# First softmax attention of a two-block transformer kernel: TensorE's order of work, item by item against two items at a time

## The reference, cut to what matters

```python
def sliding_window_attention(q, k, v, sinks):
    # 8 heads of 64 in q, 2 in k and v; blocks of 128 queries; block n sees key blocks n-1 and n
    scores = jnp.einsum('bnqhgd,bnkhd->bnhgqk', qb, kb).astype(jnp.float32) * (Dh ** -0.5)
    scores = jnp.where(valid[None, :, None, None], scores, -jnp.inf)
    m = jnp.maximum(jnp.max(scores, axis=-1, keepdims=True), sink)
    e = jnp.exp(scores - m)
    denom = jnp.sum(e, axis=-1, keepdims=True) + jnp.exp(sink - m)
    probs = (e / denom).astype(v.dtype)
    out = jnp.einsum('bnhgqk,bnkhd->bnqhgd', probs, vb)
```

## Time and profile before

| | us |
|---|---|
| three runs | 2562.1, 2562.7, 2562.7 (median 2562.7) |
| span of the profiled execution, first to last instruction | 2561.3 |
| what lies around the span (median less span) | 1.4 |
| PE busy in the span | 2541.6 |
| DVE busy in the span | 1596.4 |
| ACT busy in the span | 912.6 |
| the stage changed: first scores to last value products | 434.78 to 494.93 |
| mean granted TensorE clock | 1.000 |

### The profile page before, as it was taken

The page is one execution under the profiler, slowest core; times in us unless marked ns, Lnnn a source line. Parts: engine busy times, 40 slices in busy tenths (PEclk is TensorE's granted clock), DMA queues, the critical chain, the costliest instruction groups (busy, mean ns, idle before and its releaser), DMA issues.

```text
span 2561.3 us, 31974 instructions
## 1 busy us (share of the span) xinstructions
PE 2541.6 (99%) x12548; PEld 2107.0 (82%) x12548; DVE 1596.4 (62%) x1976; ACT 912.6 (36%) x1184; POOL 10.2 (0%) x24
## 2 busy tenths in 40 slices
PE   8999999999999999999999999999999999999999
PEld 7888888778888888877898888888886888888887
DVE  6444468866444468677765747476357665775755
ACT  5222234543222245344443423233146343432322
POOL 0000001000000000000000000000000000000000
PEclk9999999999999999999999999999999999999999
DMA  5222233112222232212321232323210232232222
GB/s 182 102 83 99 96 110 120 67 50 96 103 89 98 99 115 101 99 50 99 132 94 63 104 103 82 115 83 123 94 66 13 87 116 83 84 115 83 101 96 82
DMA packets 37410, 241.91 MB, mean 94 GB/s; under 512 B 4416, under 2 KB 7280, under 8 KB 9136
## 3 DMA queue, kind: packets, MB, share of 16 engines
q1 hardware_dynamic: 34736, 233.78, 26.3%
q10 hardware_dynamic: 1920, 5.22, 0.6%
q0 software_dynamic: 640, 1.31, 0.2%
HBM read 236.89 MB, written 2.10 MB: 93 GB/s over the span
## 4 chain that ended last, share of the span: by engine, by line
PE 93%; DVE 5%; ACT 1%; issue 1%; DMA 0%; POOL 0%; DVEq 0%; ACTq 0%
PE ps L605 24%; PE ps L607 24%; PE ps L606 24%; PE ps L1234 1%; PE ps L623 1%; PE ps L625 1%; PE ps L624 1%; PE ps L766 1%; PE ps L1267 1%; PE ps L1291 1%; PE ps L1282 1%; DVE w_lo L2048 1%; PE ps L768 1%; PE ps L767 1%; PE ps L1303 1%
## 5 line engine op out<-in xcount | busy, mean ns | idle before, releaser
L605 PE MATMUL ps<-op_hi,w_hi 128*128 128x512 f32 x2056 | 800.9, 390 | 0.2 <-DVE op_lo L1929 0.2
L606 PE MATMUL ps<-op_lo,w_hi 128*128 128x512 f32 x2056 | 800.5, 389 | 0.0
L607 PE MATMUL ps<-op_hi,w_lo 128*128 128x512 f32 x2056 | 800.4, 389 | 0.0
L1350 ACT ACTIVATE w_hi<-w_raw 128x2048 fp32r<-128x2048 f32 x217 | 414.4, 1911 | 485.2 <-PE ps L607 315.3
L2048 DVE TENSOR_TENSOR w_lo<-w_raw,w_hi 128x2048 fp32r<-128x2048 f32 x217 | 497.0, 2292 | 38.7 <-ACT w_hi L1350 22.3
L605 PEld LDWEIGHTS ps<-op_hi,w_hi 128*128 128x128 f32 x2056 | 386.3, 188 | 81.4 <-issue 1.4
L607 PEld LDWEIGHTS ps<-op_hi,w_lo 128*128 128x128 f32 x2056 | 386.2, 188 | 80.6
L606 PEld LDWEIGHTS ps<-op_lo,w_hi 128*128 128x128 f32 x2056 | 386.3, 188 | 80.3
L2013 DVE SCALAR_TENSOR_TENSOR x<-ps,x 128x512 f32<-128x512 f32 x134 | 92.7, 691 | 310.8 <-PE ps L607 293.0
L605 PE MATMUL ps<-h_hi,w_hi 128*128 128x512 f32 x692 | 269.5, 389 | 0.0
L606 PE MATMUL ps<-h_lo,w_hi 128*128 128x512 f32 x692 | 269.2, 389 | 0.0
(11 more groups left out here) (373 smaller groups left out, 3085.7 us busy)
## 6 DMA issues: line engine op xcount, KB each, us to landing
w_raw<-in_wstream_dram SPq DMA_DIRECT2D x217, 1024.0 KB, 4.8
cr_m<-in_mem_dram ACTq DMA_DIRECT2D x2, 1024.0 KB, 4.9
w_raw<-in_wstream_dram SPq DMA_DIRECT2D x7, 256.0 KB, 8.0
x<-in_x_dram SPq DMA_DIRECT2D x3, 512.0 KB, 7.3
out_dram<-x SPq DMA_DIRECT2D x3, 512.0 KB, 2.6
m_s<-m_q POOLq DMA_DIRECT2D x16, 64.0 KB, 2.5
ev_s<-in_alibi_dram ACTq DMA_DIRECT2D x1, 1024.0 KB, 4.9
m_c<-in_rope_dram ACTq DMA_DIRECT2D x1, 640.0 KB, 3.9
```

The lines of the kernel that those rows point to most:

```text
L605: mm_(o, w_hi[:, c % 4, w], hi[:, k, 0:cols], start=(k == 0), stop=False)
L606: mm_(o, w_hi[:, c % 4, w], lo[:, k, 0:cols], start=False, stop=False)
L607: mm = mm_(o, w_lo[:, c % 4, w], hi[:, k, 0:cols], start=False, stop=(k == kt - 1))
L1350: f_(w_hi[:, c % 4, :], w_raw[:, c % 2, :], ACT.Copy).then_inc(w_hi_ready, 1)
```

## The change

PE's order in this attention alone is replaced. It takes the items in pairs: the score products of items i and i+1 in one run, then the masks of both, then the turns of item i-2, an eighth of a slab, the turns of item i-1, the next eighth, and last the value products of items i-2 and i-1 in one run. The scores of a pair wait until the exponentials of both items before are done. The eighth of step 18 follows at the end. The program of DVE, ACT, POOL and SP is unchanged, and so is the number of instructions of each kind on PE. The other user of `attention` (the differential attention) keeps its order.

```diff
-                    if i not in late:
-                        between(i)
+                    between(i)
...
-                    if i in late:
-                        between(i)
+                n["it"] += N
+
+            def attention_by_pairs(slabs, items, score_parts, p_blocks, outputs, turn_bank, between):
+
+
+                i0, N = n["it"], len(items)
+                pe.wait_ge(rs_used, n["job"])
+
+                def turn(i):
+                    pe.wait_ge(p_ready, i0 + i + 1)
+                    if i == 0:
+                        pe.wait_ge(acc_free, slabs + 2)
+                    else:
+                        pe.wait_ge(pt_copied, i0 + i)
+                    for b, src in enumerate(p_blocks(i0 + i, *items[i])):
+                        mm = nc.tensor.transpose(ps[:, turn_bank, b * P:(b + 1) * P], src, ident)
+                    mm.then_inc(pt_ready, 1)
+
+                for i in range(0, N + 2, 2):
+                    if i < N:
+                        if i:
+                            pe.wait_ge(e_ready, i0 + i)
+                        pair = [score_parts(i + a, *items[i + a]) for a in range(2)]
+                        for parts in pair:
+                            for o, l, r, _ in parts:
+                                mm_(o, l, r, start=True, stop=False, skip_group_check=True)
+                        for parts in pair:
+                            for o, _, _, bias in parts:
+                                mm = mm_(o, ident_r[:], bias, start=False, stop=True, skip_group_check=True)
+                            mm.then_inc(s_ready, 1)
+                    if i:
+                        turn(i - 2)
+                    between(i)
+                    if i:
+                        turn(i - 1)
+                    between(i + 1)
+                    if i:
+                        for a in range(i - 2, i):
+                            pe.wait_ge(pt_copied, i0 + a + 1)
+                            outputs(i0 + a, *items[a])
                 n["it"] += N
...
-            attention(AT_MIX1 + MIX1_FIRST, SLIDE_ITEMS, slide_scores, slide_blocks, slide_out, [2],
-                      slide_between, late=(8, 16))
+            attention_by_pairs(AT_MIX1 + MIX1_FIRST, SLIDE_ITEMS, slide_scores, slide_blocks, slide_out, 2,
+                               slide_between)
+            slide_between(len(SLIDE_ITEMS) + 2)
```

More of the change, by code:

```diff
@@ L801, in eighth_positions, with attention @@
                     mm.then_inc(slab_done, 1)
-            def attention(slabs, items, score_parts, p_blocks, outputs, turn_banks, between, scored=None, late=()):
+            def attention(slabs, items, score_parts, p_blocks, outputs, turn_banks, between, scored=None):
                 i0, N, T = n["it"], len(items), len(turn_banks)
```

## The result

The changed kernel takes 2572.2 us (median of 5 runs, 2571.7 to 2573.1), the kernel before 2562.7 (2561.6 to 2562.9): ratio 1.0039, 95% interval 1.0027 to 1.0051. It is 9.5 us slower, 10.4 were forecast.

What follows compares the result with a forecast made beforehand. PE is nearly full, with DVE working off a backlog; pairing makes each pair one trip through PE, DVE and ACT. The stage ends 10.4 us later: 2561.3 + 10.4 = 2571.7 span, plus 1.4 gives 2573.1 us, range 2567 to 2577.

Steps and rivals of the forecast that it cites:

- What bounds the stage: In the changed stage, PE runs ahead and DVE follows with a backlog, waiting for scores only 4.4 us in all.
- 5.0 us of changes of shape: On PE alone in the stage, shape changes fall from 9.6 to 4.6 us, a gain if PE's order set the pace.
- rival A: Faster: PE sets the pace in the stage and DVE loses at most its 4.4 us of waits; 2558.3 us, chance 0.05.
- The new dependency: PE scores a pair only after the products of i-1, needing ACT's copy after the exponentials of i+1; DVE's backlog goes.
- The loop's terms: One pair's trip through PE, DVE and ACT: 7.19 us for four-block pairs, 6.65 with a one-block item first.
- plain pair: A four-block pair without other work in its loop: one trip through three engines, 7.19 us.
- other work inside the loop: DVE's work at even steps and ACT's `high` lengthen their pairs, by 0.72 to 2.25 us a piece.
- The loop's start: First pair starts at 434.78, second at 441.20 after item 1's exponentials; PE waits 2.3 us there.
- Nothing later has a known slack: Behind the stage nothing absorbs the delay, so the levels and all after run some 10 us later.
- rival C: Slower still: PE, idle more, is granted 1.2 GHz through the stage; 2609 us, chance 0.03.
- second loop of nearly the same length: The turn of i-1, waiting for the copy of i-2, closes another loop, within 0.2 us; up to 1.4 more in total.
- Rival B: No difference that can be told: DVE's idle 7.1 us behind the stage takes up lateness; 2566.0 us, chance 0.06.

Runs made afterwards that it cites:

- products_by_two: The kernel before, item order kept, with only the value products taken two items in a row at every second step: 2561.3 us, ratio 0.9998.
- wait_only: The kernel before, item order kept, with scores of an even item waiting for the exponentials of the item just before: 2568.2 us, ratio 1.0022.
- products_later: The changed kernel with a pair's value products moved behind the next pair's scores: 2566.6 us, ratio 1.0017.
- change_filled: The changed kernel with 34 unread matmuls of 512 columns added in PE's waits: 2572.4 us, ratio 1.0039.
- besides_odd: The changed kernel with three pieces of DVE's other work moved one step later, out of the loop: 2569.6 us, ratio 1.0030.
- dve_by_pairs: The changed kernel with DVE by pairs too, probabilities of i-1 first, then the maxima of i and i+1: 2568.7 us, ratio 1.0025.
- all_by_pairs: The changed kernel with DVE ordered by pairs, ACT's other work moved, and value products behind the next pair's scores: 2563.5 us, ratio 1.0004.
- masks_apart: The changed kernel with each item's masks right behind its own scores, sixteen more changes of shape: 2572.5 us, ratio 1.0038.

## Why the prediction was right, point by point

- **What bounds the stage.** Right. The 5.0 us of changes of shape were PE's to win and DVE's pace gave nothing for them. In products_by_two 1.2 to 2.8 of them (an estimate) were taken without a new dependency, and 0.4 us of the stage came of it; the rest, fewer runs of scores and masks, was not tried without the dependency. The Trainium skill, "TensorEngine Tiling (Array Packing)", section Key Properties, says that a change of tiling mode drains the engine. The 0.15 to 0.20 us per change of the earlier trace rows agree with it; the gain that follows from it alone, rival A, did not come.
- **The new dependency.** Right, and shown apart: wait_only has the wait for the exponentials in the item order and loses, products_later takes copy and products out of it in the pair order and wins 5.6 us back.
- **The loop's terms.** The plain pair was put at 7.19; with full clock it is 7.20 (change_filled). The price that the trace of before did not show, 0.21 for two more score matmuls in a long run, is (1.06 - 0.63) / 2 = 0.215: eight cost 1.06 us in the chain of the changed kernel at 471.68, four 0.63. The other work inside the loop (1.25, 0.72, 1.29, 2.18, 2.25) gave each of the five pairs that have it right to 0.1. These are sums: that each piece counts in full only while nothing else is longer is what besides_odd showed.
- **The loop's start.** 6.42 forecast and measured; the tail from the last maxima 13.10 forecast, 12.98 measured (491.65 to 504.63).
- **Beyond the stage.** "Nothing later has a known slack" held: from the first product for the levels to the end 2067.1 us after, 2067.7 before.
- **What was off.** Three things. The clock: rival C was taken as PE at 1.2 GHz for the whole stage, with a chance of 0.03, and 5 us for a spell in one pair; two spells came, and cost 0.5 and 0.1. PE's waits: 16 to 18 us were forecast, the longest ahead of the products; the PE lines for DVE's and ACT's results come to 11.5 us (5.7 ahead of the products, 3.7 of the turns, 2.1 of the scores), and the longest is the 2.08 before the second pair. And the "second loop of nearly the same length" was named only through the turn of i-1; the loop that besides_odd and dve_by_pairs ran into is ACT's own work at odd steps, as long as 7.9 to 8.5 where `to_end` and `high` stand. In the changed kernel ACT came from `to_end` to the exponentials of item 7 at 461.17, just when DVE's maxima of item 7 were done (461.13), so the term that was left out cost nothing there. That is luck: nothing in the prediction compared the two. My expectation for dve_by_pairs left ACT out again and was twice too large.
- **The size.** 10.4 forecast, 9.5 measured by the medians, 9.2 in the two profiled executions: 10.8 more in the stage, 0.96 less ahead of it and 0.6 less behind it. The 0.4 by which the stage is over the forecast is the spell in the second pair (0.5), less 0.1 in the tail. The start of the stage scatters by 2 us between the thirteen executions, so the nearness of 9.5 to 10.4 says less than the lengths of the pairs do.
- **Rival B** (the levels take the lateness up) did not come: the stretch behind the stage kept its length.

## What to carry to other kernels

Before making runs longer on one engine, follow one item through all the engines and count how many items are in flight. Here pairing halved PE's changes of shape, but it also made the scores of a pair wait for the last step of the pair before; a backlog of one item on the next engine was worth more than all 5 us of shape changes. Where an order is changed on one engine, the others' orders have to be changed with it: with DVE and ACT reordered and the products moved, the same pairs came back level with the kernel before (2563.5), but no further: DVE was busy for 50.5 us of the stage before and for 50.4 in all_by_pairs, and its 4.6 us of waits had become 5.7 in other places.

## What the runs showed of the hardware that was not expected

- The same wait was followed by half the clock in some executions and not in others. The PE wait of 1.85 us between 1890 and 1904 stands in identical code in all thirteen profiled executions: behind it the granted clock was 0.50 for 3.4 us in five, for 6.8 in products_by_two, and 1.00 in seven, the kernel before among them. In the stage, a wait of 2.08 us (the changed kernel, 440) was followed by windows of 0.77, 0.50 and 0.87, one of 1.98 (masks_apart, 479) by three of 0.50, and one of 1.65 at the place of the first (wait_only) by 1.00 throughout. The same program can do both: the eleven runs of products_by_two have mean clocks from 0.998 to 1.000.
- What a spell cost depended on what the loop was waiting for. It was 0.5 us in the second pair of the changed kernel (7.66 against 7.20 with filler), nothing in the second pair of all_by_pairs (6.91 against 6.90), where DVE set the length, and in masks_apart the two pairs with spells were 2.3 us longer than with filler. There 27 unread matmuls in the waits kept 1.00 and made the stage 1.7 us shorter, with the 0.6 that they cost in other pairs.
